# Reordering the launch of a two-block transformer kernel: first weights behind the constants, five row groups first, the norm's root and the distance tables elsewhere

## The reference

```python
mod = silu(c) @ w_ada + b_ada             # 1024 -> 3 x 1024: shift, scale, gate
h = rms_norm(x, norm_gain) * (1 + scale) + shift
proj = h @ w_in                           # queries, keys, values and gates of two attentions
# A: windowed attention with a relative-position bias (rel_bias by distance bucket) and sinks
# B: keys and values compressed in blocks of 32 by a small MLP, selected and windowed branches
x = x + gate * (attention_output @ w_out)
```

## Time and profile before

| | |
|---|---|
| median of 3 runs | 1768.63 us (1764.9, 1768.63, 1775.61) |
| profiled execution | 1764.49 us |
| its span | 1762.7 us |
| TensorE busy | 1692.0 us (96%) |
| VectorE busy | 976.5 us (55%) |
| ScalarE busy | 679.9 us (39%) |
| DMA | 202.02 MB, mean 115 GB/s |

### The profile page before, as it was taken

How to read it: one execution, slowest core, us unless ns; L and a number is a source line. 1 busy time by engine, 2 the same in 40 slices (tenths; PEclk the granted TensorE clock), 3 DMA queues, 4 the chain that set the end, 5 groups by cost and what they waited for, 6 DMA issues and landing times.

```text
span 1762.7 us, 23061 instructions
## 1 busy us (share of the span) xinstructions
PE 1692.0 (96%) x8968; PEld 1407.7 (80%) x8968; DVE 976.5 (55%) x1803; ACT 679.9 (39%) x1417; POOL 61.4 (3%) x119
## 2 busy tenths in 40 slices
PE   4999999999999999899999999999999899999999
PEld 2777777777999999777888888887888788888887
DVE  4666566656867777676555555336555633333332
ACT  3334555554545555564332323223222433333221
POOL 0000000000000000000000000000000000000000
PEclk9899998999999999998999999998999899999999
DMA  8886333212323131311566665343443233333332
GB/s 304 212 247 167 108 85 95 74 37 68 72 58 99 48 97 38 95 49 48 169 179 180 189 191 162 110 120 86 120 131 96 72 96 97 100 100 98 94 116 78
DMA packets 290216, 202.02 MB, mean 115 GB/s; under 512 B 76248, under 2 KB 272073, under 8 KB 289083
## 3 DMA queue, kind: packets, MB, share of 16 engines
q1 hardware_dynamic: 266942, 133.21, 27.1%
q0 software_dynamic: 15536, 56.37, 10.6%
q10 hardware_dynamic: 7628, 10.97, 1.9%
HBM read 197.33 MB, written 5.28 MB: 115 GB/s over the span
## 4 chain that ended last, share of the span: by engine, by line
PE 89%; DVE 5%; ACT 2%; DMA 2%; issue 1%; ACTq 1%; SPq 0%; DVEq 0%
PE PS L860 13%; PE PS L862 13%; PE PS L861 13%; PE PS L842 4%; PE PS L843 4%; PE PS L844 4%; PE PS L1285 3%; PE PS L1287 3%; PE PS L1286 3%; PE PS L1090 3%; PE PS L1335 2%; PE PS L1359 2%; PE PS L1064 2%; PE PS L1072 1%; PE PS L1347 1%
## 5 line engine op out<-in xcount | busy, mean ns | idle before, releaser
L2016 DVE TENSOR_TENSOR WL<-WS,WH 128x512 fp32r<-128x512 f32 x416 | 268.1, 686 | 256.2 <-ACT WH L1508 255.7
L1508 ACT ACTIVATE WH<-WS 128x512 fp32r<-128x512 f32 x416 | 237.7, 621 | 178.0 <-PE PS L844 135.0
L860 PE MATMUL PS<-A3H,WL 128*128 128x512 f32 x672 | 262.9, 391 | 0.1
L862 PE MATMUL PS<-A3H,WH 128*128 128x512 f32 x672 | 261.7, 389 | 0.0
L861 PE MATMUL PS<-A3L,WH 128*128 128x512 f32 x672 | 261.4, 389 | 0.0
L860 PEld LDWEIGHTS PS<-A3H,WL 128*128 128x128 f32 x672 | 126.1, 188 | 30.0 <-issue 4.4
L862 PEld LDWEIGHTS PS<-A3H,WH 128*128 128x128 f32 x672 | 126.1, 188 | 26.6
L861 PEld LDWEIGHTS PS<-A3L,WH 128*128 128x128 f32 x672 | 126.2, 188 | 25.8
L842 PE MATMUL PS<-GH,WL 128*128 128x512 f32 x352 | 137.4, 390 | 0.6 <-DVE WL L2016 0.6
L844 PE MATMUL PS<-GH,WH 128*128 128x512 f32 x352 | 137.0, 389 | 0.0
L843 PE MATMUL PS<-GL,WH 128*128 128x512 f32 x352 | 137.0, 389 | 0.0
(11 more groups left out here) (362 smaller groups left out, 3492.8 us busy)
## 6 DMA issues: line engine op xcount, KB each, us to landing
AW<-in_ada_w POOLq DMA_DIRECT2D x96, 512.0 KB, 4.2
WS<-in_ffn_w_gate_up SPq DMA_DIRECT2D x88, 512.0 KB, 4.3
WS<-in_ffn_w_down SPq DMA_DIRECT2D x32, 512.0 KB, 4.2
WS<-in_sc_w_in SPq DMA_DIRECT2D x24, 512.0 KB, 4.2
AB<-in_w_ada SPq DMA_DIRECT2D x8, 1024.0 KB, 16.0
WS<-in_w_in SPq DMA_DIRECT2D x32, 256.0 KB, 4.2
WS<-in_diff_w_qkv SPq DMA_DIRECT2D x64, 128.0 KB, 2.7
WS<-in_ffn_w_down SPq DMA_DIRECT2D x16, 384.0 KB, 3.6
```

Source lines behind the costliest of these rows:

```text
L860: mm(PS[:, b, :], wl[:, k, :], hi[:, k, 0:S], start=(k == 0), stop=False)
L862: m = mm(PS[:, b, :], wh[:, k, :], hi[:, k, 0:S], start=False, stop=(k == KT - 1))
L1508: f(weights(p)[0][:, k, :], WS[:, p % 2, k, :], ACT.Copy).then_inc(w_hi, 1)
L2016: tt(lo[:, k, :], WS[:, p % 2, k, :], hi[:, k, :].bitcast(F32), ALU.subtract).then_inc(w_lo, 1)
```

## The change

The order of the launch is another on every engine.

- SP issues the eight blocks AB right behind CN. HOT and RB go to ACT's queue; SP issues no small rows.
- Five groups of rows (c, c_2, c_ctx_2, b_ada, norm_gain) go into a tile EARLY of their own, issued first on ACT, ahead of XS; TensorE turns them alone, VectorE copies them, and CS is made from them. Of the other 19 groups GpSimd issues 10 (after clearing VEC), ACT 9, behind CS.
- TensorE turns the other rows and multiplies RB by HOT after the squares, in PSUM banks 3 to 6; ScalarE, not VectorE, copies them out.
- ScalarE makes the norm's root right after the squares; then these four copies, the issue of the distance rows, GBB, GD and the sinks; then the splits of the two kcvc panels; then the high parts of the layer norm. The distance table is issued after the layer norm, ahead of z0's split.
- The modulation's second half (the scale) is multiplied and summed first, in bank 2; VectorE adds bias and gain to it while the shift's half is summed. The six small gains and products stand behind the layer norm.

```diff
 STAGES = [
+    ("mods0", 1, 0, 0, 1, 0),
     ("x_in", 1, 0, 8, 0, 0),
-    ("mods1", 1, 0, 0, 4, 0),
...
+        def early_rows_in(eng):
+
+            for v, src in small_rows()[:N_EARLY]:
+                eng.dma_start(EARLY[v:v + src.shape[0], :], src).then_inc(early_in, 16)
+
+        def rows_in(eng, share, done):
+
+            for v, src in small_rows()[N_EARLY + share::2]:
...
         @block.sync
         def _(sp):
             sp.dma_start(CN[:, :], consts[:, 0:C_KEEP]).then_inc(const_in, 16)
-            sp.wait_ge(vec_zero, 1)
-            rows_in(sp, 0)
-            sp.dma_start(HOT[:, :], consts[0:34, C_HOT:C_HOT + 640]).then_inc(row_in, 16)
-            sp.dma_start(RB[0:32, :], ins["rel_bias"]).then_inc(row_in, 16)
-            sp.dma_start(RB[32:34, :], consts[32:34, C_HEAD:C_HEAD + 16]).then_inc(row_in, 16)
-
             w_ada = ins["w_ada"][0].rearrange("(k p) n -> k p n", p=P)
...
+            pool.wait_ge(vec_zero, 1)
+            rows_in(pool, 0, pool_rows)
+
             pool.wait_ge(cs_ready, 1)
...
-            a = At("mods1")
-            pe.wait_ge(vec_in, 16 * len(small_rows()))
-            for k in range(2):
-                take_small(a, k)
-                tp(PS[:, SMALL, 0:P], VEC[:, k, :], IDENT).then_inc(small_done, 1)
...
+            a = At("mods0")
+            pe.wait_ge(early_in, 16 * N_EARLY)
+            take_small(a, 0)
+            tp(PS[:, SMALL, 0:V_N1], EARLY[:, :], IDENT[0:V_N1, 0:V_N1]).then_inc(small_done, 1)
             pe.wait_ge(x_in, 16)
...
             add_square(KT - 1)
+            n = len(small_rows()) - N_EARLY
+            pe.wait_ge(pool_rows, 16 * ((n + 1) // 2))
+            pe.wait_ge(vec_in, 16 * (n // 2))
+            for k in range(2):
+                tp(PS[:, 3 + k, 0:P], VEC[:, k, :], IDENT).then_inc(rows_turned, 1)
+            pe.wait_ge(row_in, 48)
+            for k in range(2):
+                mm(PS[0:16, 5 + k, 0:320], RB[:, :], HOT[:, k * 320:(k + 1) * 320], start=True, stop=True).then_inc(rows_turned, 1)
             a = At("ada_a")
             take_small(a, 0)
-            for half in range(2):
-                pe.wait_ge(ada_used, 2 * KT - 2 + half)
+            for n, half in enumerate((1, 0)):
+                pe.wait_ge(ada_used, 2 * KT - 2 + n)
                 for f in range(KT):
...
+                m.then_inc(ada_sums if half else small_done, 1)
...
+            early_rows_in(act)
             act.dma_start(XS[:, :, :], ins["x"][0].rearrange("(t p) d -> p t d", p=P)).then_inc(x_in, 16)
-            act.wait_ge(vec_zero, 1)
-            rows_in(act, 1)
-
...
+            act.dma_start(HOT[:, :], consts[0:34, C_HOT:C_HOT + 640]).then_inc(row_in, 16)
...
             f(CS[:, :], VT[:, V_C:V_C + 24], ACT.Silu).then_inc(cs_ready, 1)
+            act.wait_ge(vec_zero, 1)
+            rows_in(act, 1, vec_in)
...
-            a = At("mods1")
-            act.wait_ge(small_free, a.small(3) + 1)
+            load_set(LN_AND_EXP)
+            root(At("norm_a"), 0, RS[:, 0, :], 1.0 / D, ln_rs, S)
+            for k in range(2):
+                act.wait_ge(rows_turned, k + 1)
...
+            act.wait_ge(rows_taken, 4)
             act.dma_start(dist_rows, US[:, :]).then_inc(rows_out, 16)
+            act.dma_start(GBB[:, :], ins["b_nsa_gate"].rearrange("o n -> (o n)").partition_broadcast(P)).then_inc(extra_in, 16)
...
+            for j in range(2):
+                split(At("kcvc"), j)
+            act.wait_ge(small_free, At("ada_a").small(0) + 1)
+            layer_norm(None, 0, A1H, slice(0, S), M1)
 
             act.wait_ge(rows_out, 16)
             for head, at, n in ((0, 3 * P - 1, 2 * P), (8, P - 1, S)):
                 act.dma_start(dist_table[head:head + 8, :, 0:n],
...
-            load_set(LN_AND_EXP)
-            layer_norm("norm_a", 0, A1H, slice(0, S), M1, first_panels=At("kcvc"))
...
+            a = At("mods0")
+            dve.wait_ge(small_done, a.small(0) + 1)
+            copy(VT[:, 0:V_N1], PS[:, SMALL, 0:V_N1]).then_inc(small_free, 1)
+            dve.wait_ge(cs_ready, 1)
+            add_ada()
+            split(At("kcvc"), 0)
+            split(At("kcvc"), 1)
+            dve.wait_ge(ada_sums, 1)
+            tt(M1[:, 8:16], PS[:, SMALL - 5, 0:8], VT[:, V_BADA + 8:V_BADA + 16], ALU.add).then_inc(ada_scale, 1)
...
+            layer_norm(0, None, H, A1H, A1L, slice(0, S), None, M1[:, 0:8], None, 0)
+            dve.wait_ge(rows_taken, 2)
```

More of the change, by code:

```diff
@@ L34 @@
 NGATE = 24
+N_EARLY = 5
 V_BADA, V_C, V_C2, V_CC, V_NG, V_N1, V_N2, V_CONV = 0, 24, 32, 40, 48, 56, 72, 88
@@ L460, in hybrid_then_diff_conv @@
         FLAT = PS[:, :, :].rearrange("p b s -> p (b s)")
+        early_in, rows_turned, rows_taken, ada_sums = (sem(n) for n in ("early_in", "rows_turned", "rows_taken", "ada_sums"))
+        ada_scale, pool_rows = sem("ada_scale"), sem("pool_rows")
         const_in, x_in, vec_in, row_in, ctx_in, rope_in, extra_in = (sem(n) for n in (
@@ L650, in rows_in @@
                     dst = VEC[r:r + src.shape[0], k, 0:src.shape[1]]
-                eng.dma_start(dst, src).then_inc(vec_in, 16)
+                eng.dma_start(dst, src).then_inc(done, 16)
         @block.sync
@@ L1543, in wait_norm, with layer_norm @@
                     eng.wait_ge(nrm_out, a.norm(n) - 1)
-            def layer_norm(stage, L, dst, tok, bias, n=S, first_panels=None, tiles=range(KT)):
-                if 0 in tiles:
+            def layer_norm(stage, L, dst, tok, bias, n=S, tiles=range(KT)):
+                if stage is not None:
                     root(At(stage), 0, RS[:, 0, 0:n], 1.0 / D, ln_rs, n)
-                if first_panels is not None:
-                    for j in range(2):
-                        split(first_panels, j)
                 for k in tiles:
@@ L1554, in layer_norm @@
                     f(dst[:, k, tok], RAW[:, k % 2, 0:n], ACT.Identity, bias=bias[:, k:k + 1]).then_inc(ln_hi, 1)
+            early_rows_in(act)
             act.dma_start(XS[:, :, :], ins["x"][0].rearrange("(t p) d -> p t d", p=P)).then_inc(x_in, 16)
-            act.wait_ge(vec_zero, 1)
-            rows_in(act, 1)
[L1560 to L1566, removed]
-            a = At("mods1")
+            act.dma_start(HOT[:, :], consts[0:34, C_HOT:C_HOT + 640]).then_inc(row_in, 16)
+            act.dma_start(RB[0:32, :], ins["rel_bias"]).then_inc(row_in, 16)
+            act.dma_start(RB[32:34, :], consts[32:34, C_HEAD:C_HEAD + 16]).then_inc(row_in, 16)
+            a = At("mods0")
             act.wait_ge(small_free, a.small(0) + 1)
             f(CS[:, :], VT[:, V_C:V_C + 24], ACT.Silu).then_inc(cs_ready, 1)
+            act.wait_ge(vec_zero, 1)
+            rows_in(act, 1, vec_in)
             a = At("x_in")
@@ L1579, in _ @@
                 f(H[:, k, :], PS[:, b, :], ACT.Copy).then_inc(acc_free[b], 1)
-            a = At("mods1")
-            act.wait_ge(small_free, a.small(3) + 1)
-            act.dma_start(dist_rows, US[:, :]).then_inc(rows_out, 16)
+            load_set(LN_AND_EXP)
+            root(At("norm_a"), 0, RS[:, 0, :], 1.0 / D, ln_rs, S)
+            for k in range(2):
+                act.wait_ge(rows_turned, k + 1)
+                c = slice(V_N1, P) if k == 0 else slice(0, P)
+                f(VT[:, k * P + c.start:k * P + c.stop], PS[:, 3 + k, c], ACT.Copy).then_inc(rows_taken, 1)
+            for k in range(2):
+                act.wait_ge(rows_turned, 3 + k)
+                f(US[:, k * 320:(k + 1) * 320], PS[0:16, 5 + k, 0:320], ACT.Copy).then_inc(rows_taken, 1)
+            act.wait_ge(rows_taken, 4)
+            act.dma_start(dist_rows, US[:, :]).then_inc(rows_out, 16)
+            act.dma_start(GBB[:, :], ins["b_nsa_gate"].rearrange("o n -> (o n)").partition_broadcast(P)).then_inc(extra_in, 16)
+            for which, name in enumerate(("diff_q_norm_2", "diff_k_norm_2")):
+                for half in range(2):
+                    src, dst = ins[name][0], GD[:, which, 32 * half:32 * half + 32]
+                    act.dma_start(view(dst, [16, 2], [1, 16]),
+                                  bass.AP(src.tensor, src.offset + 16 * half, [[0, P], [32, 2], [1, 16]])).then_inc(extra_in, 16)
+            act.dma_start(SINK[:, :], ins["sinks"].rearrange("o n -> (o n)").partition_broadcast(P)).then_inc(extra_in, 16)
+            for j in range(2):
+                split(At("kcvc"), j)
+            act.wait_ge(small_free, At("ada_a").small(0) + 1)
+            layer_norm(None, 0, A1H, slice(0, S), M1)
             act.wait_ge(rows_out, 16)
@@ L2073, in add_ada @@
                         dve.wait_ge(ada_used, 2 * k - 1)
-                        for half in range(2):
+                        for half in (1, 0):
                             c = slice(D * half, D * (half + 1))
@@ L2127, in _ @@
                    ALU.mult).then_inc(lam_mul, 1)
[L2128 to L2135, removed]
             a = At("kcvc")
```

28 lines of the change are left out of this document (10 added, 18 removed).

## The result

The changed kernel took 1773.12 us (median of 20 runs), the one before 1766.66 us (20 runs). The ratio is 1.0032, 95% interval 1.0018 to 1.0046: the change makes the kernel some 5.7 us slower (3 to 8). The profiled execution took 1772.5 us for a span of 1770.7 us, 8.0 more than before.

A forecast was written before the change was run, and what follows sets the result against it. TensorE, busy 96% of the span, bounds the kernel; only its waits lose time. Launch gain of 6.3 us against the table's 5 to 6 on top of 11 gives +5 on 1766.8: 1771 us, range 1759 to 1780.

The forecast's parts named there:

- signs named beforehand: Changed profile: last product ends at 32 to 33 us, XS lands at 17 to 21, norm 40 to 46, hidden product 93 to 96.
- Weights first: Launch, AB issued on SP right behind CN: last block there at 30 us, products end at 32.6 instead of 40.35.
- x beside AB: Launch, XS beside AB: queues take turns by packet; XS lands at 18.5 to 19 us, squares end at 31 to 31.6.
- ScalarE's row: Launch, ScalarE behind the root: copies, seven issues to 38.9 us, first splits to 42.0, norm at 42.9 (40 to 46).
- The table's issue: Behind the norm, ahead of z0's split: two issues take 4.2 us, z0 split at 58.2, TensorE waits 1.6 us.
- The full stretch: z2's issue to z3's landing, DMA engines full: 16.7 + 6.3 = 23.0 us, z3 lands at 83.3, 4.3 us later.
- the chain is the same: Behind z3 and T: unchanged 10.9 us from landing to the first hidden product.
- TensorE then full: From the first hidden product on: TensorE is full.
- the gain was not kept: Rival, full stretch: table's write finds gaps, or T and z3 do not wait for it; 1760.5 us, chance 0.27.
- Turns by equal bytes: Rival, DMA queues: turns hold equal bytes, z3 in at about 80, shift -1 to +1 us; 1767, chance 0.12.
- the fourth rival: T copies behind the table: slower by over 1%, z3's low half 18 to 22 us late; 1786 us, chance 0.05.

The follow-up runs named there:

- second part later: Kernel with x first and table on GpSimd behind the rows, but the table's second part (2 MB) issued by ScalarE at some 140 us; ratio 0.9985.

## Why the prediction was right

The forecast was +5 us, the measurement 6.5 in the medians and 5.7 in the ratio. The sign and the mechanism were right: the price of the table's move outweighs what the launch gives. In the old launch that is shown, where the move alone gives 1.0032; with x first, the kernel with the table behind the norm (1.0015) is 0.36% slower than the one with it ahead of the splits (0.9979). In the changed kernel's own launch it is not told apart (1.0032 against 1.0026). That the size came out is in good part luck. The launch gave 3.6 us for 6.3; the way from the norm to the hidden product cost 12.1 us more than before, for 11.3; so the shift at the hidden product was 8.5 us and not 5. Then 3.2 us of it were gone by the compressed sum, where the forecast had put nothing. Of the signs named beforehand these came: the norm's start, z3's issue (63.9) and nearly its landing (85.8 for 82 to 85). These did not: the last product, x, the squares, TensorE's wait ahead of z0, VectorE's wait for T, and the hidden product. The 1% that I took for the least that can be measured was too much: twenty runs of each tell 0.3%. By its steps:

- *Weights first.* Products ended at 34.9, not 32.6. CS stood at 9.9 (9.2 foreseen), but AB's blocks landed some 2.4 us later than 0.41 MB/us from 2.5 us on had made them.
- *x beside AB.* The rule was right, and one turn was as long as worked out: 313 packets of ScalarE's queue in 15 to 23 us are 0.41 us each per engine, for 0.42. The landing was mis-sized, 23.2 for 19: x's packets had all but none of the first 5 us (ScalarE's queue moved 16 packets in 2 to 5 us), and HOT, RB and the rows took turns of their own. The squares, by ScalarE's last copy into H as there, ended at 35.0, not 31.6.
- *ScalarE's row.* The seven issues took 3.4 us as foreseen; the sums were at 4.17 us near the fast end. The norm at 45.6 lay in the range (40 to 46), 2.7 us above the 42.9 worked out; x, 4 us late, more than accounts for it.
- *The table's issue* took 2.43 us, not 4.2, so z0's split ended before the first projections did (61.3), and TensorE did not stand in front of z0. The 1.6 us that I saw there did not come.
- *The full stretch.* I added engine times (16.7 + 6.3 = 23.0 us) and let z3 be the late one. It landed at 85.8 (foreseen 83.3), but the one that TensorE waited for first was z2: issued at 60.5 (foreseen 60.3), it took 20.5 us to land. T was there when VectorE came (83.3; foreseen 82), if by less than 1 us, and z3's low half was done at 88.2 (87). The hidden product came at 98.4, above the 93 to 96, because the next issue and the hidden weights' landing (6.71 us for 4.09) were slow too. Why z2 took so long is shown in part. With three queues busy the counts were nearly equal, so each 256 B packet of q1 waited for two larger ones; in 66 to 70 us:

```profile
q0 software_dynamic: 253, 0.94, 62.1%
q10 hardware_dynamic: 221, 0.45, 29.0%
q1 hardware_dynamic: 219, 0.06, 6.2%
```

- *The rest of z2's 20.5 us.* In 62 to 66 us the counts were not equal (1226 of q1, 553 of q10), though the engines were 96% busy. So equal turns do not explain all of it, and the rest stays open.
- *What came back.* The shift of 8.5 us at the hidden product is only 5.3 us at the compressed sum (171.7 for 166.4). "TensorE then full" was right, but not "the chain is the same": in the kernel before, the granted clock was below full from 130 to 150 us, in the changed kernel not. Windows of the kernel before (us, PE, PEld, DVE, ACT, POOL busy, PEclk, DMA share, GB/s):

```profile
130.00:140.00 10.00, 10.00 (x57) 8.57 (x56) 6.22 (x10) 2.60 (x4) 0.08 (x1) 0.90 0.68 155
140.00:150.00 10.00, 10.00 (x46) 7.96 (x46) 5.83 (x8) 4.68 (x8) 0.98 (x2) 0.93 0.71 215
```

and of the changed kernel:

```profile
130.00:140.00 10.00, 10.00 (x52) 7.31 (x51) 6.63 (x7) 2.84 (x4) 0.53 (x1) 1.00 0.93 240
140.00:150.00 10.00, 10.00 (x65) 8.76 (x64) 7.14 (x11) 3.46 (x6) 0.53 (x1) 1.00 0.45 108
```

That is 1.7 us of the 3.2, as far as one execution of each can tell. It is not shown to belong to the change: of the fourteen profiles seven have a granted clock of 0.93 or less in a 10 us window between 130 and 150 us, and seven have none. From 172 us to the end the shift of the two profiled executions grew again by 2.7 us, to 8.0. There the mean granted clock of 175 to 300 us was 0.90 for 0.93, which is up to 3.8 us; but the two fastest kernels have 0.90 too, so this as well is no effect of the change that the traces show.

The rivals: the gain was not kept; another order, with x first and the table on GpSimd, is 6.2 us faster than the kernel before, and that this is near the 6.3 named is chance. Turns by equal bytes are out: 182 packets of 8 KB passed beside 179 of 4 KB, and 567 beside 567 of 64 B. The rule quoted beside them from the Trainium skill ("DMA: Bandwidth & Descriptors", "Queues, rings and completion order") is another one, since it counts a turn in descriptors and not in bytes, and equal counts alone do not speak against it: turns of a dozen descriptors on either side would give them too. What speaks against it is the order of the packets, one of each queue by turns (505 of 526 turns), if a packet of the profile is taken as one descriptor. Of the fourth rival only the mechanism was half there: a T copy blocked ScalarE for 9.7 us, but in the changed kernel T was not what VectorE waited for, and the table on another queue cost as much.

The prediction had a hole beside its success: it credited 6.3 us of the norm to the reordering as a whole. Most of the 3.6 us that it got, the table's move alone would have given.

## What to carry to other kernels

A transfer that nobody waits for still has a price, and it is paid by whatever small-packet transfer runs beside it: put it into a stretch where nobody waits for such a transfer, and look for the panel that will be in flight there, not only for the queue that it stands on. When a wait or an issue is moved off an engine, ask what was queued behind it; it may be worth more than the part the change is named for. And in a launch bound by bytes, order the loads by what each starts: x in front of the weights cost the weights 0.3 us and gave the norm 4 us. Last, a sum that comes out right is not yet a model that is right: here two misses of 3 us each had opposite signs.

## What the runs showed of the hardware

- The DMA engines took turns by packet with equal counts at very different sizes: 182 against 179 (8 KB beside 4 KB), 265 against 269 (both 4 KB), 567 against 567 (8 KB beside 64 B). Halving one load's packets gave its neighbour half as much rate again. Equal counts are not the rule everywhere: 1226 against 553 (256 B beside the table's packets, 62 to 66 us).
- An issue on ScalarE's queue can stand for long when much is queued: 9.7 us for a T copy and 8.45 us for GBB (12 KB), both right behind the table; the same T copy took 0.56 us when the table was on GpSimd at the same moment. SyncE stood 8.3 us at an issue of z3.
- Beside the table, a panel of small packets landed 15 to 22 us after its issue, whether that was at 37, 41, 51, 61 or 138 us; without it, z3's took 11.8 (kernel before, behind the table) and 11.7 us (second part later).
- The 32 sums of one column each took 6.96 to 6.99 us at a granted clock of 0.50, after TensorE had stood for 5 to 11 us, and 4.17 us at 1.00, when it had been busy up to them.
